# One projection stage by groups of 512 tokens, in place of two stages by tiles of 128

## The chip, the cores and the metric

The kernel runs on one core of a Trainium2 chip. The metric is the device time of one execution in microseconds (us). Engines are named as in the profile: PE is the matrix engine, PEld its weight loads, DVE the vector engine, ACT the scalar engine, POOL the general one, SP the queue that issues most transfers.

## What is computed

One layer of a decoder trunk: 2048 tokens of width 1024, token mixing, cross-attention to 256 memory tokens, a mixture of 32 experts, a final norm. All is float32. The change touches the projection ahead of the token mixing and the first of the two mixings:

```python
h = rmsnorm(x, norm_mix)              # (2048, 1024)
z = h @ w_in                          # (1024, 5 * 512): u, v_a, q, k, v
y_a = gelu(u) * (tril(w_s) @ rmsnorm(gelu(v_a), v_gain) + b_s)   # within chunks of 128 tokens, 4 groups of 128 channels
y_b = stick_breaking_attention(q, k, v)                          # 8 heads of 64, causal
x = x + concat(rmsnorm(y_a, out_norm_a), rmsnorm(y_b, out_norm_b)) @ w_out
```

## The kernel before

Every float32 product is made of three fp32r matmuls (`split_product`, L56 to L60): both operands are split into a high part (rounded to fp32r, by ACT) and a low part (the rest, by DVE), and high x high, high x low and low x high are added up in PSUM. A product of 128 tokens by 512 columns over the depth of 1024 is 8 x 3 = 24 matmuls of 128x512.

The work around the change stands in stages, each a block of its own with its own semaphores and an all-engine barrier behind it (`Scope.close`):

- `project_qkv` (L74 on) runs over 16 tiles of 128 tokens: load x, square (ACT), root (POOL), scale (DVE), 8 transposes of the normed tile (L286), split into `h_hi` and `h_lo`, then the products q, k and v with the tokens stationary and the weights moving. The result has tokens on the partitions, and the attention wants q and k with features there, so q and k are split, transposed head by head with both parts side by side (8 transposes at L315, 8 at L323), copied by ACT and DVE together and stored to DRAM by runs of 128 tokens. All 6 MB of the q, k and v weights are held, split, in SBUF.
- `mix_chunks` (L335 on) runs over the 16 tiles again: it loads and norms x, transposes (L598) and splits it a second time, makes the products u and v_a (the weights' 4 MB are loaded and cut at its start), gelu (ACT), the group norm (DVE, POOL), the spatial mix (4 matmuls at L614), gate, norm and store. The first loads of the attention (`StickLoads.load_first`) are issued near its end.
- `attend_stick` follows and loads q, k and v from DRAM by chunks of 512 tokens, with one transfer for each head of a pair.

Within a stage each engine has its order written out by hand, and waits on counting semaphores.

Of the kernel before, what the change touches and what calls it, by code (L numbers as in the profile page):

```python
# [6 lines left out]
ACT = mybir.ActivationFunctionType  # L7
# [13 lines left out]
class Scope:  # L21
# [15 lines left out]
    def two_views(self, name, shape):  # L37

        at = -(-self.nc.sbuf_base // 32) * 32
        cut = self.sbuf(name, shape, F32R)  # L40
        return cut, self.nc.alloc_sbuf_tensor_at(f"{self.stage}_{name}_raw", shape, F32, offset=at)
# [27 lines left out]
def project_qkv(nc, x, gain, w_in, ident, half, ident_bf, above, qt, kt, v):  # L69


    tokens, width = x.shape
    tiles, rows = tokens // P, width // P
    first_col = w_in.shape[1] - 3 * BANK  # L74
    heads, head_dim = qt.shape[0], qt.shape[1] // 2
    cols = w_in.shape[1] - first_col
    with ExitStack() as stack:
        s = Scope(nc, stack, "qkv")
        w_hi = s.sbuf("w_hi", [P, rows, cols], F32R)
        w_lo, w_raw = s.two_views("w_lo", [P, rows, cols])  # L80
        gains = s.sbuf("gains", [P, width])
        xs = s.sbuf("xs", [P, 2, width])
        hs = s.sbuf("hs", [P, 2, width])
        junk = s.sbuf("junk", [P, width], BF16)
        stat = s.sbuf("stat", [P, 2, 4])
        h_hi = s.sbuf("h_hi", [P, 2, rows, P], F32R)
        h_lo = s.sbuf("h_lo", [P, 2, rows, P], F32R)
        q_parts = s.sbuf("q_parts", [P, heads, 2, head_dim], F32R)
        k_parts = s.sbuf("k_parts", [P, heads, 2, head_dim], F32R)
        q_t = s.sbuf("q_t", [P, 2, heads, P], F32R)  # L90
        k_t = s.sbuf("k_t", [P, 2, heads, P], F32R)
        v_out = s.sbuf("v_out", [P, 2, BANK])
        ht_ps = s.psum("ht_ps", [P, rows, P])
        z_ps = s.psum("z_ps", [P, 3, BANK])
        t_ps = s.psum("t_ps", [P, heads, P])

        w_loaded = [[s.sem(f"w_loaded{c}_{r}") for r in range(rows)] for c in range(3)]
        filled, masked = s.sem("filled"), s.sem("masked")
        gains_loaded = s.sem("gains_loaded")
        w_hi_done, w_lo_done = s.sem("w_hi_done"), s.sem("w_lo_done")  # L100
        x_loaded = [s.sem(f"x_loaded{i}") for i in range(2)]
        squared, meaned, rooted, h_done = s.sem("squared"), s.sem("meaned"), s.sem("rooted"), s.sem("h_done")
        ht_done, hh_done, hl_done = s.sem("ht_done"), s.sem("hh_done"), s.sem("hl_done")
        zq_done, zk_done, zv_done = s.sem("zq_done"), s.sem("zk_done"), s.sem("zv_done")
        q_hi, q_lo, k_hi, k_lo = s.sem("q_hi"), s.sem("q_lo"), s.sem("k_hi"), s.sem("k_lo")
        qt_done, kt_done = s.sem("qt_done"), s.sem("kt_done")
        qt_act, qt_dve, kt_act, kt_dve = s.sem("qt_act"), s.sem("qt_dve"), s.sem("kt_act"), s.sem("kt_dve")
        v_done = s.sem("v_done")
        stored = [s.sem(f"stored{i}") for i in range(2)]
        half_heads = heads // 2  # L110

        with nc.Block() as block:
            @block.sync
            def _(sp):
                def load_x(t, slot):
                    sp.dma_start(xs[:, slot], x[bass.ds(t * P, P), :]).then_inc(x_loaded[slot], 16)

                def load_w(c):
                    for r in range(rows):
                        sp.dma_start(w_raw[:, r, c * BANK:(c + 1) * BANK],  # L120
                                     w_in[r * P:(r + 1) * P, first_col + c * BANK:first_col + (c + 1) * BANK]).then_inc(w_loaded[c][r], 16)

                load_x(0, 0)
                load_w(0)
                load_x(1, 1)
                load_w(1)
                load_w(2)

                def store(t, slot):
                    sp.wait_ge(qt_act, t + 1)  # L130
                    sp.wait_ge(qt_dve, t + 1)
                    sp.dma_start(qt[:, :, bass.ds(t * P, P)].rearrange("h p t -> p h t"), as_f32(q_t[:, slot])).then_inc(stored[slot], 16)
                    sp.wait_ge(v_done, t + 1)
                    sp.dma_start(v[bass.ds(t * P, P), :], v_out[:, slot]).then_inc(stored[slot], 16)
                    sp.wait_ge(kt_act, t + 1)
                    sp.wait_ge(kt_dve, t + 1)
                    sp.dma_start(kt[:, :, bass.ds(t * P, P)].rearrange("h p t -> p h t"), as_f32(k_t[:, slot])).then_inc(stored[slot], 16)

                with sp.Fori(0, tiles // 2 - 1) as j:
                    for slot in range(2):  # L140
                        sp.wait_ge(h_done, 2 * j + slot + 1)
                        load_x(2 * j + slot + 2, slot)
                        store(2 * j + slot, slot)
                for slot in range(2):
                    store(tiles - 2 + slot, slot)
                for slot in range(2):
                    sp.wait_ge(stored[slot], 16 * 3 * tiles // 2)

            @block.gpsimd
            def _(pool):  # L150
                def root(t, slot):
                    pool.wait_ge(meaned, t + 1)
                    nc.gpsimd.tensor_tensor(stat[:, slot, 2:3], stat[:, slot, 1:2], half[:, 0:1], ALU.pow).then_inc(rooted, 1)

                nc.gpsimd.memset(ident[:], 0.0).then_inc(filled, 1)
                nc.gpsimd.memset(half[:], -0.5).then_inc(filled, 1)
                nc.gpsimd.memset(ident_bf[:], 0.0).then_inc(filled, 1)
                nc.gpsimd.memset(above[:], 0.0).then_inc(filled, 1)
                pool.wait_ge(filled, 4)
                for tile, compare, fill in ((ident, ALU.not_equal, 1.0), (ident_bf, ALU.not_equal, 1.0), (above, ALU.is_gt, -1e30)):  # L160
                    nc.gpsimd.affine_select(out=tile[:], in_=tile[:], compare_op=compare, fill=fill, base=0,
                                            pattern=[[-1, P]], channel_multiplier=1).then_inc(masked, 1)
                root(0, 0)
                with pool.Fori(0, tiles // 2 - 1) as j:
                    root(2 * j + 1, 1)
                    root(2 * j + 2, 0)
                root(tiles - 1, 1)

            @block.scalar
            def _(act):  # L170
                def square(j, slot):

                    act.wait_ge(x_loaded[slot], 16 * (j + 1))
                    nc.scalar.activation(junk[:], xs[:, slot], ACT.Square, accum_out=stat[:, slot, 0:1]).then_inc(squared, 1)

                def high_h(t, slot):
                    act.wait_ge(ht_done, t + 1)
                    for part in range(2):
                        last = nc.scalar.copy(h_hi[:, slot, 4 * part:4 * part + 4], ht_ps[:, 4 * part:4 * part + 4])
                    last.then_inc(hh_done, 1)  # L180

                def cut_w(c):
                    for r in range(rows):
                        act.wait_ge(w_loaded[c][r], 16)
                        nc.scalar.copy(w_hi[:, r, c * BANK:(c + 1) * BANK], w_raw[:, r, c * BANK:(c + 1) * BANK]).then_inc(w_hi_done, 1)

                act.dma_start(gains[:], gain.partition_broadcast(P)).then_inc(gains_loaded, 16)
                square(0, 0)
                cut_w(0)
                high_h(0, 0)  # L190
                cut_w(1)
                cut_w(2)

                def tile(j, slot, last_tile=False):
                    t = 2 * j + slot
                    if not last_tile:
                        square(j + slot, 1 - slot)
                    act.wait_ge(zq_done, t + 1)
                    wait_past(act, qt_done, t)
                    nc.scalar.activation(q_parts[:, :, 0, :], z_ps[:, 0].rearrange("p (h d) -> p h d", h=heads),  # L200
                                         ACT.Copy, scale=head_dim ** -0.5).then_inc(q_hi, 1)
                    if not last_tile:
                        high_h(t + 1, 1 - slot)
                    act.wait_ge(zk_done, t + 1)
# [2052 lines left out]
```

## Time and profile before

| | us |
|---|---|
| median of 3 runs | 2894.77 (2889.86 to 2895.51) |
| profiled execution | 2895.18 |
| its span, first to last instruction | 2893.4 |
| `project_qkv`, first to last matmul or transpose | 9.6 to 334.3 |
| `mix_chunks`, first to last matmul | 351.1 to 585.0 |
| first matmul of the attention | 592.2 |

Over the span PE is busy for 91%, PEld 72%, DVE 52%, ACT 46% and POOL 22%, and PE's granted clock is 0.953 of full speed. Starts in the rows are counted from the first instruction. The end of a matmul in a row is modelled, so that neighbours overlap: what one costs is read from start to start.

### The profile page before, as it was taken

What the parts mean: (1) busy time and instruction counts of PE and PEld (TensorE: products, weight loads), DVE (VectorE), ACT (ScalarE), POOL (GpSimd) and SP (SyncE); (2) the same over time, 40 slices, a digit from 0 to 9 for tenths busy, and PEclk for the clock granted to TensorE, in tenths of its full rate; (3) what the DMA queues carried; (4) which work ended last, traced back from release to release, by engine and by line L of the source; (5) the groups of instructions that cost most, each with busy time, mean ns of one, the idle gap of its engine ahead of it and who ended that gap; (6) DMA issues with size and microseconds to landing.
All of it is one profiled execution on the core that took longest, in us unless ns stands there. A gap on an engine that the chain in (4) does not pass through costs nothing. (4 is left out here: it accounts for less than half of the span.)

```text
span 2893.4 us, 46489 instructions
## 1 busy us (share of the span) xinstructions
PE 2622.1 (91%) x14633; PEld 2095.4 (72%) x14635; DVE 1493.9 (52%) x1975; ACT 1316.4 (45%) x2332; POOL 629.1 (22%) x697
## 2 busy tenths in 40 slices
PE   7999689979999979978999999949999999999991
PEld 6888578856667657757678888737777788888880
DVE  4222245578888862220433333265788855555643
ACT  4222233278989961100322222124777755555642
POOL 0000011157777730000000000031222211112223
PEclk9999899989999989989999999959999999999995
DMA  4333411242021022232312221143999966666856
GB/s 167 94 91 94 135 61 59 62 89 67 16 67 49 2 88 98 101 141 104 114 53 78 87 80 59 66 170 118 372 372 367 355 217 210 208 213 219 282 152 249
DMA packets 203097, 406.93 MB, mean 141 GB/s; under 512 B 26096, under 2 KB 67568, under 8 KB 202992
## 3 DMA queue, kind: packets, MB, share of 16 engines
q1 hardware_dynamic: 186576, 363.04, 36.1%
q0 software_dynamic: 13968, 33.59, 5.0%
q10 hardware_dynamic: 2448, 8.91, 0.8%
q8 instruction: 64, 1.05, 0.2%
q14 instruction: 41, 0.34, 0.0%
HBM read 339.39 MB, written 83.36 MB: 146 GB/s over the span
## 5 line engine op out<-in xcount | busy, mean ns | idle before, releaser
L746 POOL TENSOR_TENSOR stick_weight<-stick_weight,stick_left 128x512 f32<-128x512 f32 (+3 forms) x320 | 327.9, 1038 | 127.0 <-DVE stick_left L874 122.6
L1625 DVE TENSOR_TENSOR moe_w_lo<-moe_w_lo_raw,moe_w_hi (+1 forms) x256 | 297.7, 1220 | 57.6 <-ACT moe_w_hi L1621 51.8
L1621 ACT CAST moe_w_hi<-moe_w_lo_raw (+1 forms) x256 | 255.2, 1054 | 39.3 <-DMA moe_w_lo_raw<-in_w 29.3
L874 DVE TENSOR_TENSOR_SCAN stick_left<-stick_z_ps,stick_left,stick_any_row 128x512 f32<-128x512 f32 x192 | 240.3, 1276 | 35.4 <-ACT stick_z_ps L837 35.1
L835 ACT ACTIVATE stick_weight<-stick_z_ps 128x512 f32<-128x512 f32 (+3 forms) x320 | 173.6, 542 | 32.7 <-PE stick_z_ps L784 21.1
L797 PE MATMUL stick_t_ps<-all_ident,stick_weight 128*128 128x128 f32 x1088 | 165.2, 281 | 18.8 <-ACT stick_weight_t L844 9.2
L58 PE MATMUL exp_g_ps<-moe_w_hi,exp_x_hi 128*128 x376 | 154.7, 411 | 22.0 <-DVE moe_w_lo L1625 11.1
L837 ACT ACTIVATE stick_z_ps<-stick_z_ps 128x512 f32<-128x512 f32 (+3 forms) x320 | 165.7, 518 | 10.4
L797 PEld LDWEIGHTS stick_t_ps<-all_ident,stick_weight 128*128 128x128 f32 x1088 | 116.1, 141 | 69.7 <-issue 45.6
L58 PE MATMUL qkv_z_ps<-qkv_w_hi,qkv_h_hi 128*128 128x512 f32 x384 | 157.5, 410 | 4.0 <-DVE qkv_h_lo L238 4.0
L58 PE MATMUL exp_y_ps<-moe_w_hi,exp_h_hi 128*128 128x512 f32 x376 | 153.5, 408 | 2.3 <-DVE exp_h_lo L2054 2.3
L2058 DVE TENSOR_TENSOR moe_w_lo<-moe_w_lo_raw,moe_w_hi 128x1024 f32 (+1 forms) x128 | 148.3, 1219 | 12.9 <-ACT moe_w_hi L2020 10.0
L59 PE MATMUL qkv_z_ps<-qkv_w_lo,qkv_h_hi 128*128 128x512 f32 x384 | 152.9, 398 | 0.0
L1636 POOL DMA_INDIRECT moe_xg<-hm_scratch,moe_now x50 | 60.6, 1212 | 423.1 <-PE exp_x_ps L2069 420.2
L60 PE MATMUL qkv_z_ps<-qkv_w_hi,qkv_h_lo 128*128 128x512 f32 x384 | 152.5, 397 | 0.0
L59 PE MATMUL exp_g_ps<-moe_w_lo,exp_x_hi 128*128 x376 | 150.1, 399 | 0.0
L60 PE MATMUL exp_g_ps<-moe_w_hi,exp_x_lo 128*128 x376 | 150.0, 399 | 0.0
L59 PE MATMUL exp_y_ps<-moe_w_lo,exp_h_hi 128*128 x376 | 149.4, 397 | 0.0
L60 PE MATMUL exp_y_ps<-moe_w_hi,exp_h_lo 128*128 128x512 f32 x376 | 149.3, 397 | 0.0
L58 PE MATMUL exp_u_ps<-moe_w_hi,exp_x_hi 128*128 x376 | 148.7, 395 | 0.0
L59 PE MATMUL exp_u_ps<-moe_w_lo,exp_x_hi 128*128 x376 | 148.7, 395 | 0.0
L60 PE MATMUL exp_u_ps<-moe_w_hi,exp_x_lo 128*128 x376 | 148.5, 395 | 0.0
(287 smaller groups left out, 5934.9 us busy)
## 6 DMA issues: line engine op xcount, KB each, us to landing
moe_w_lo_raw<-in_w SPq DMA_DIRECT2D x512, 256.0 KB
moe_w_lo_raw<-in_w SPq DMA_DIRECT2D x128, 512.0 KB
qkv_xs<-in_x SPq DMA_DIRECT2D x16, 512.0 KB, 4.7
qt_scratch<-qkv_q_t SPq DMA_DIRECT2D x16, 512.0 KB, 3.2
kt_scratch<-qkv_k_t SPq DMA_DIRECT2D x16, 512.0 KB, 3.5
gmlp_xs<-in_x SPq DMA_DIRECT2D x16, 512.0 KB, 3.7
mix_q<-qt_scratch SPq DMA_DIRECT2D x32, 256.0 KB
out_xs<-in_x SPq DMA_DIRECT2D x16, 512.0 KB, 3.4
```

Of the source, the lines that this page charges most:

```text
L58: pe.matmul(out, left_hi, right_hi, start=first, stop=False)
L59: pe.matmul(out, left_hi, right_lo, start=False, stop=False)
L60: return pe.matmul(out, left_lo, right_hi, start=False, stop=last)
L746: nc.gpsimd.tensor_tensor(taken, taken, after, ALU.mult).then_inc(weight_done, 1)
L797: last = nc.tensor.transpose(t_ps[:, n % 2, b], weight[:, n % W_SLOTS, b * P:(b + 1) * P], ident)
L835: nc.scalar.activation(weight[:, n % W_SLOTS, 0:keys], z, ACT.Sigmoid).then_inc(take_done, 1)
L837: nc.scalar.activation(z, z, ACT.Sigmoid, scale=-1.0).then_inc(leave_done, 1)
L874: nc.vector.tensor_tensor_scan(row[:, c * BANK:c * BANK + keys][:, ::-1], back, any_row[:, 0:keys], start, ALU.mult, ALU.bypass).then_inc( ...
L1621: nc.scalar.copy(self.w13_hi[:, self.w13_at(e, i)], self.w13_raw[:, self.w13_at(e, i)]).then_inc(self.w13_cut, 1)
L1625: ops.tensor_tensor(self.w13_lo[:, self.w13_at(e, i)], self.w13_raw[:, self.w13_at(e, i)], as_f32(self.w13_hi[:, self.w13_at(e, i)]), ALU. ...
L1636: nc.gpsimd.indirect_dma_start(out=self.xg[:], out_offset=None, in_=self.hm, in_offset=bass.IndirectOffsetOnAxis(ap=self.now[:].bitcast(U3 ...
L2058: nc.vector.tensor_tensor(w2_lo[:, w2_at(e, i)], w2_raw[:, w2_at(e, i)], as_f32(w2_hi[:, i]), ALU.subtract).then_inc(w2_ready, 1)
```

## The change

The two stages become one, `project`, without a loop: the order is a list of steps that every engine walks through.

- The steps are ("turn", t), the transposes and the split of tile t, and units, one product of 24 matmuls each. Tokens are taken by groups of 512 ("quads", 4 of them). `h_hi` and `h_lo` hold two quads.
- v is made by tokens as before. q and k are made by features: 128 columns of the weights are stationary and the 512 tokens move, so the result has features on the partitions, ACT and DVE split it straight into `qk_out`, and no transposes of q and k are left. Their scratch tensors are laid out by pairs of heads, and a store has runs of 512 tokens.
- A first pass makes q, k and v for all quads (48 units). The split tokens of quads 0 and 1 are written to DRAM on the way (`park`, 2 transfers of 2 MB for each quad); those of quads 2 and 3 stay.
- A gate pass makes u and v_a by tiles of 128 tokens (32 units) and the mixing, from quad 3 down to quad 0. It fetches the parked tokens again. x is loaded, normed and transposed once.
- The u and v_a weights are loaded over those of q and k during the first pass; those of v lie where the attention's first chunks come later (`room`). Products go round 4 PSUM banks.
- `StickLoads` loads both heads of a pair with one transfer over 128 partitions.

```diff
+    order = [("turn", 0), ("turn", 1)]
+    for a in range(per):
+        order.append((V, 0, a))
+        if a + 2 < per:
+            order.append(("turn", a + 2))
+    for quad in range(quads):
+        products = [(c, quad, f) for c in ((Q, K, V) if quad == quads - 1 else (Q, K) if quad == 0 else (V, Q, K)) for f in range(per)]
+        turns = [("turn", per * (quad + 1) + a) for a in range(per)] if quad < quads - 1 else []
+        for n, product in enumerate(products):
+            order.append(product)
+            if turns and n % (len(products) // per) == 0:
+                order.append(turns.pop(0))
+    gate_tiles = [per * quad + a for quad in range(quads - 1, -1, -1) for a in range(per)]
+    Z_SLOTS, X_SLOTS, OUT_SLOTS = 4, 3, 3
...
 SP, in the walk through the order
+                    if step == (K, quads - 1, 0):
+                        sp.wait_ge(z_done, number[(Q, quads - 1, per - 1)] + 1)
+                        load_w(U)
+                    if step == (V, quads - 1, 0):
+                        sp.wait_ge(z_done, number[(K, quads - 1, per - 1)] + 1)
+                        load_w(G)
...
+                    if n:
+                        store(n - 1)
+                    if step in ((Q, 0, 2), (Q, 1, 2)):
+                        park(step[1])
...
+                for m in range(tiles):
+                    if m == per:
+                        sp.wait_ge(z_done, n_units + 2 * per)
+                        sp.wait_ge(parked_out[1], 32)
+                        fetch(1)
...
 ACT
+                    if quad >= 2 and t % per == 0:
+                        act.wait_ge(z_done, 3 * per * (quad - 1))
+                        act.wait_ge(parked_out[quad % 2], 32)
...
+                square(0)
+                cut_w(V, range(rows // 2))
+                for step in order:
+                    if step[0] == "turn":
+                        t = step[1]
+                        high_h(t)
+                        if t == 0:
+                            cut_w(V, range(rows // 2, rows))
+                            square(1)
+                        if t + 2 < tiles:
+                            square(t + 2)
+                        if t == 2:
+                            cut_w(Q, range(rows))
+                        if t == 3:
+                            cut_w(K, range(rows))
+                        continue
+                    take(number[step])
+                    if step == (K, quads - 1, per - 1):
+                        cut_w(U, range(rows))
+                    if step == (V, quads - 1, 1):
+                        cut_w(G, range(rows))
...
 PE
-                    for h in range(heads):
-                        last = nc.tensor.transpose(t_ps[:, h], as_f32(q_parts[:, h].rearrange("p a d -> p (a d)")), ident)
-                    last.then_inc(qt_done, 1)
...
+                        last = split_product(nc.tensor, z_ps[:, n % Z_SLOTS], w_hi[i][:, r, cols], w_lo[i][:, r, cols],
+                                             h_hi[:, quad % 2, r], h_lo[:, quad % 2, r], r == 0, r == rows - 1)
...
+                for m, t in enumerate(gate_tiles):
+                    n, quad = n_units + 2 * m, t // per
+                    if quad < 2 and t % per == 0:
+                        pe.wait_ge(parked_in[quad % 2], 32)
+                    by_tokens(n, t, U, m == 0)
...
+                    by_tokens(n + 1, t, G, m == 0)
...
+                    if m:
+                        mix(m - 1)
```

ACT at the start, before. `xs` is the tile of x, `w_hi` the high part of the weights, `h_hi` that of the transposed tile:

```order
L174 ACTIVATE qkv_junk,qkv_stat<-qkv_xs 128x1024
L185 CAST qkv_w_hi<-qkv_w_lo_raw 128x512 x8
L179 CAST qkv_h_hi<-qkv_ht_ps 128x512 x2
L185 CAST qkv_w_hi<-qkv_w_lo_raw 128x512 x16
L174 ACTIVATE qkv_junk,qkv_stat<-qkv_xs 128x1024
L200 ACTIVATE qkv_q_parts<-qkv_z_ps 128x8x64
```

ACT at the start, in the change:

```order
L301 ACTIVATE proj_junk,proj_stat<-proj_xs 128x1024
L318 CAST proj_w_hi_54<-proj_w_lo_raw 128x512 x4
L311 CAST proj_h_hi<-proj_ht_ps 128x4x128 x2
L318 CAST proj_w_hi_54<-proj_w_lo_raw 128x512 x4
L301 ACTIVATE proj_junk,proj_stat<-proj_xs 128x1024 x2
L311 CAST proj_h_hi<-proj_ht_ps 128x4x128 x2
L301 ACTIVATE proj_junk,proj_stat<-proj_xs 128x1024
L326 COPY proj_v_out<-proj_z_ps 128x512
```

The first weights are cut in two halves around the first tile, and the tiles 1 and 2 are squared ahead of the other weights, which come between the first products.

PE at the seam between the two stages before: the last transposes of k, the transposes of the spatial weights, those of the first tile, and the first product of u.

```order
L60 MATMUL qkv_z_ps<-qkv_w_hi,qkv_h_lo 128x512
L323 MATMUL qkv_t_ps<-all_ident,qkv_k_parts 128x128 x8
...
L619 MATMUL gmlp_mix_ps<-all_ident,gmlp_ws_raw 128x128 x4
L598 MATMUL gmlp_ht_ps<-all_ident,gmlp_hs 128x128 x8
L58 MATMUL gmlp_z_ps<-gmlp_w_hi,gmlp_h_hi 128x512
```

PE at the seam between the two passes in the change, behind the first product of u:

```order
L67 MATMUL proj_z_ps<-proj_w_hi,proj_h_lo 128x512
L541 MATMUL proj_mix_ps<-all_ident,proj_ws_raw 128x128 x4
L65 MATMUL proj_z_ps<-proj_w_hi,proj_h_hi 128x512
L66 MATMUL proj_z_ps<-proj_w_lo,proj_h_hi 128x512
...
L519 MATMUL proj_mix_ps<-proj_v_norm,proj_ws_t 128x128 x4
```

Products stand right behind products here; only the 4 transposes of the spatial weights lie between.

SP's queue in the loop over the tiles, before:

```order
L116 DMA qkv_xs<-in_x 128x1024
L132 ISA
L132 DMA qt_scratch<-qkv_q_t 128x8x128
L134 ISA
L134 DMA v_scratch<-qkv_v_out 128x512
L137 DMA kt_scratch<-qkv_k_t 128x8x128
```

SP's queue around the first parking, in the change:

```order
L178 DMA proj_xs<-in_x 128x1024
L194 DMA qt_scratch<-proj_qk_out 128x2x512 x2
L200 DMA parked_scratch<-proj_h_hi 128x4096
L200 DMA parked_scratch<-proj_h_lo 128x4096
L178 DMA proj_xs<-in_x 128x1024
L194 DMA qt_scratch<-proj_qk_out 128x2x512 x2
```

The two large stores stand between the store of one q unit and the next load of x.

## Rows read from the trace of the kernel before

**Rows 1.** By stretch: length, busy us of PE, PEld, DVE, ACT, POOL; clock, DMA, GB/s

```profile
15.50:333.50 318.00, 313.19 (x1523) 257.80 (x1523) 92.66 (x139) 86.03 (x153) 8.21 (x15) 0.99 0.32 96
333.50:369.30 35.80, 3.93 (x21) 2.92 (x19) 14.72 (x16) 15.13 (x19) 1.72 (x3) 0.54 0.69 235
369.30:576.50 207.20, 207.20 (x1000) 170.82 (x1001) 106.91 (x217) 58.34 (x115) 30.55 (x43) 0.99 0.17 55
576.50:592.20 15.70, 3.15 (x17) 2.66 (x16) 6.81 (x17) 2.21 (x6) 2.29 (x5) 0.68 0.09 34
```

**Rows 2.** Waits of PE until 592 us: total, times, longest

```profile
PE gmlp_mix_ps L619 <- POOL gmlp_ws_raw L450: 16.8, 1, 16.8
...
PE gmlp_z_ps L58 <- DVE gmlp_h_lo L536: 14.4, 1, 14.4
```

**Rows 3.** Timeline of the start: start, length, engine, line [idle before, releaser]

```profile
7.15 5.25 ACT L185 CAST qkv_w_hi<-qkv_w_lo_raw 128x512 fp32r<-128x512 f32 x8
...
9.61 1.94 PE L286 MATMUL qkv_ht_ps<-all_ident,qkv_hs 128*128 128x128 f32 x8 [9.61 <-DVE qkv_hs L231]
12.31 1.07 ACT L179 CAST qkv_h_hi<-qkv_ht_ps 128x512 fp32r<-128x512 f32 x2
...
15.54 0.80 PE L58 MATMUL qkv_z_ps<-qkv_w_hi,qkv_h_hi 128*128 128x512 f32 x1 [3.98 <-DVE qkv_h_lo L238]
...
24.44 1.05 ACT L174 ACTIVATE qkv_junk<-qkv_xs 128x1024 bf16<-128x1024 f32 x1
...
27.78 1.97 PE L286 MATMUL qkv_ht_ps<-all_ident,qkv_hs 128*128 128x128 f32 x8 [4.78 <-DVE qkv_hs L231]
29.40 0.78 PE L58 MATMUL qkv_z_ps<-qkv_w_hi,qkv_h_hi 128*128 128x512 f32 x1
```

**Rows 4.** Timeline of PE in `project_qkv`: one product and the transposes behind it

```profile
153.82 0.48 PE L58 MATMUL qkv_z_ps<-qkv_w_hi,qkv_h_hi 128*128 128x512 f32 x1
154.14 0.39 PE L59 MATMUL qkv_z_ps<-qkv_w_lo,qkv_h_hi 128*128 128x512 f32 x1
154.37 0.39 PE L60 MATMUL qkv_z_ps<-qkv_w_hi,qkv_h_lo 128*128 128x512 f32 x1
...
159.50 1.03 PE L323 MATMUL qkv_t_ps<-all_ident,qkv_k_parts 128*128 128x128 f32 x8
```

**Rows 5.** Timeline of PE at the seam of the two stages

```profile
333.28 1.03 PE L323 MATMUL qkv_t_ps<-all_ident,qkv_k_parts 128*128 128x128 f32 x8
...
369.27 0.76 PE L58 MATMUL gmlp_z_ps<-gmlp_w_hi,gmlp_h_hi 128*128 128x512 f32 x1 [14.36 <-DVE gmlp_h_lo L536]
...
377.13 1.04 PE L598 MATMUL gmlp_ht_ps<-all_ident,gmlp_hs 128*128 128x128 f32 x8
```

**Rows 6.** Timeline of PE in `mix_chunks`: from one spatial mix to the next

```profile
434.62 1.05 PE L614 MATMUL gmlp_mix_ps<-gmlp_v_norm,gmlp_ws_t 128*128 128x128 f32 x8
...
441.13 1.03 PE L598 MATMUL gmlp_ht_ps<-all_ident,gmlp_hs 128*128 128x128 f32 x8
441.92 0.48 PE L58 MATMUL gmlp_z_ps<-gmlp_w_hi,gmlp_h_hi 128*128 128x512 f32 x1
...
447.60 1.05 PE L614 MATMUL gmlp_mix_ps<-gmlp_v_norm,gmlp_ws_t 128*128 128x128 f32 x8
```

**Rows 7.** Timeline of PE from the last product to the attention

```profile
576.52 1.05 PE L614 MATMUL gmlp_mix_ps<-gmlp_v_norm,gmlp_ws_t 128*128 128x128 f32 x8
...
592.21 0.90 PE L784 MATMUL stick_z_ps<-mix_k_first,mix_q 64*128 64x128 f32 x6 [7.27 <-PEq L32]
```

**Rows 8.** Transfers: all loads of x until 60 us; stores of q (KB, us to landing)

```profile
DMA to landing us min/median/max: 4.7/6.4/9.8
...
qt_scratch<-qkv_q_t SPq DMA_DIRECT2D x16, 512.0 KB, 3.2
```

**Rows 9.** By stretch, as rows 1: two stretches with the DMA engines full

```profile
0.00:20.00 20.00, 6.41 (x20) 5.14 (x22) 12.00 (x21) 13.98 (x24) 2.04 (x12) 1.00 0.92 335
...
600.00:620.00 20.00, 17.39 (x172) 12.23 (x172) 16.28 (x21) 17.89 (x44) 13.38 (x15) 1.00 0.97 196
```

More of the change, by code:

```diff
@@ new lines, in project @@
+    quads = tiles // per
+    pairs, head_dim = qt.shape[0], qt.shape[2] // 2
+    U, G, Q, K, V = range(5)
+    slot_of = {V: 2, Q: 0, K: 1, U: 0, G: 1}
+    cut_order = [V, Q, K, U, G]
+    order = [("turn", 0), ("turn", 1)]
[10 more added lines that the diff above has]
+                order.append(turns.pop(0))
@@ L380, in mix_chunks @@
[L380 to L384 removed]
+        w_loaded = [[s.sem(f"w_loaded{i}_{r}") for r in range(rows)] for i in range(3)]
@@ new lines, in _ @@
+                for tile, compare, fill in ((ident, ALU.not_equal, 1.0), (ident_bf, ALU.not_equal, 1.0), (above, ALU.is_gt, -1e30)):
+                    nc.gpsimd.affine_select(out=tile, in_=tile, compare_op=compare, fill=fill, base=0,
+                                            pattern=[[-1, P]], channel_multiplier=1).then_inc(masked, 1)
+                for t in range(tiles):
+                    pool.wait_ge(meaned, t + 1)
+                    nc.gpsimd.tensor_tensor(stat[:, t, 2:3], stat[:, t, 1:2], half[:, 0:1], ALU.pow).then_inc(rooted, 1)
@@ new lines, in _ @@
+                dve.wait_ge(gains_loaded, 16)
+                norm(0)
+                cut_w(V, range(rows // 2))
+                for step in order:
+                    if step[0] == "turn":
+                        t = step[1]
+                        low_h(t)
+                        if t == 0:
+                            cut_w(V, range(rows // 2, rows))
+                            norm(1)
+                        if t + 2 < tiles:
+                            norm(t + 2)
+                        if t == 2:
+                            cut_w(Q, range(rows))
+                        if t == 3:
+                            cut_w(K, range(rows))
+                        continue
+                    take(number[step])
+                    if step == (K, quads - 1, per - 1):
+                        cut_w(U, range(rows))
+                    if step == (V, quads - 1, 1):
+                        cut_w(G, range(rows))
@@ new lines, in by_tokens @@
+                def by_tokens(n, t, c, first):
+                    i, quad = slot_of[c], t // per
+                    bank_free(n)
+                    for r in range(rows):
+                        if first:
+                            pe.wait_ge(w_lo_done, cut_order.index(c) * rows + r + 1)
+                        last = split_product(nc.tensor, z_ps[:, n % Z_SLOTS], h_hi[:, quad % 2, r, in_quad(t)], h_lo[:, quad % 2, r, in_quad(t)],
+                                             w_hi[i][:, r], w_lo[i][:, r], r == 0, r == rows - 1)
+                    last.then_inc(z_done, 1)
```

737 lines of the change are left out of this document (285 added, 452 removed).

## Prediction

> **What bounds the kernel now.** I read first the busy time by stretch [rows 1], to see where PE is idle between the first instruction and the attention's first matmul at 592.2 us. In the first stage it is busy for 313 of 318 us and in the second for 207.2 of 207.2: both are bound by PE, with DVE at 29% and 52% and ACT at 27% and 28%. Between them lie 35.8 us with 3.9 us of PE, and behind them 15.7 us with 3.2 us. Then the waits of PE [rows 2]: two of them make up nearly all of the seam, 16.8 us until the spatial weights are masked and 14.4 us until the first tile is split, which stands behind the cutting of the new weights on DVE. So three things are worth something here: matmuls that go, the seam, and the start. Work taken from ACT, DVE or the DMA queues inside the stages is worth nothing.
>
> Then the price of PE's pieces, from start to start. A matmul of 128x512 takes 0.23 us (154.14 to 154.37). A product of 24 of them behind a group of small matmuls takes 159.50 - 153.82 = 5.68 us, of which 0.09 is its first step (0.32 in place of 0.23): 5.59 us where it stands behind another product [rows 4]. Eight transposes take 441.92 - 441.13 = 0.79 us, with the slow first step behind them 0.88. The spatial mix (4 matmuls of two rows each) costs 0.81 + 0.09 = 0.90. A tile of the second stage repeats after 447.60 - 434.62 = 12.98 us = 2 x 5.59 + 0.88 + 0.90 [rows 6]. The pieces add up.
>
> **The change, part by part.** I lay out PE's new order in time with these prices and compare the start of the second to last mix, 576.52 us [rows 7].
>
> *Number of matmuls.* q and k by features: 4 groups of features x 4 quads x 24 = 384 each; by tokens it was 16 x 24 = 384. Nothing changes there, nor in v, u and v_a: 80 products in all. Each matmul has its own weight load before and after, and both orders change the stationary operand two times in three. I take 5.59 us for both kinds.
>
> *q and k transposes go.* 32 groups x 0.88 = 28.2 us, all on the path. The copies behind them (ACT, DVE) go too, at no gain. The last of these groups borders on the seam and is counted there.
>
> *The second norm and transposes go.* 16 groups of 8: 15 on the path x 0.88 = 13.2 us, one in the seam.
>
> *The seam goes.* From the last k transposes to the first product of u it is 369.27 - 333.28 = 36.0 us, and that product takes 377.13 - 369.27 = 7.86 us in place of 5.68, since the granted clock has fallen meanwhile (0.54 in this stretch) [rows 1, 5]. In the change the products of u follow those of v. What covers the weights: u's are cut behind (K, 3, 3), with all of v of quad 3 (22.4 us) still to be done, against 5.25 us of cutting for 8 pieces on ACT [rows 3]. The load of the v_a weights starts at the end of (K, 3, 3) too; 2 MB took about 9.8 us at the start at worst [rows 8]; ACT comes to them behind (V, 3, 1), 11.2 us on, and is done by about 17.5, DVE by 18.6; they are wanted after 22.4 + 5.6 = 28 us. The margin is 9 us. If that cover fails, the stall is what exceeds it. The transposes of the spatial weights cost 0.5 us. Seam: 36.0 + 2.2 - 0.5 = 37.7 us.
>
> *The start.* Before, the first product starts at 15.54 us. Now PE's order has turn 1 ahead of it. ACT: half of the cuts until 7.15 + 2.6 = 9.8 us; the first transposes end at 11.55; high part 1.07 us, to 12.7; the other half, to 15.3; the square of tile 1. From a square's start to its transposes it took 27.78 - 24.44 = 3.34 us, and from those to the product 29.40 - 27.78 = 1.62 [rows 3]. So turn 1 starts at 18.7 and the first product at 20.3, 4.8 us later than before. x of tile 1 is issued at about 5.6 us and lands at 15.4 by the slowest row [rows 8], just in time. At the slow clock the first product takes up to 7.86 us (the row of the seam): end at 28.2. In return the second product waits no more: before, PE was idle for 4.78 us and transposed slowly at 27.78 [rows 3]. Then V 0, turn 2, V 1, turn 3, V 2, V 3: the cuts for q (ACT from about 31 to 37 us) are wanted at 47, those of k at 69. x of tile 3 is queued behind 6 MB of weights, lands at about 15.6 + 9.8 = 25.4 us and is wanted at 34.
>
> *Sum.* End of the first product 28.2; 79 more x 5.59 = 441.6; 14 turns x 0.88 = 12.3; spatial transposes 0.5; 14 mixes x 0.90 = 12.6: the second to last mix starts at 495.2 us against 576.5. The gain is 81.3 us. The tail of 15.7 us is the same chain (group norm, mix, gate, norm, store, barrier) and stays [rows 7].
>
> *What is queued where.* Evictions: a q or k unit costs ACT 0.6 and DVE 0.7 us of 5.6, and 4 banks give PE three more units. SP: the load of x for tile t + 3 stands behind a store that waits for the unit before. A load took 4.7 to 9.8 us [rows 8], and the tile is wanted two turns later, at least 11 us.
>
> *Parking.* This is the part without a row. 4.2 MB are written for quad 0, and again for quad 1, then read twice. Nearest rows: all engines full at 335 GB/s and at 196 GB/s [rows 9]; a store of 512 KB in 3.2 us with its latency, 164 GB/s [rows 8]. That is 12.5, 21 or 25.6 us. On the way out the cover is the queue behind it: the store of (Q, 0, 2) lands late, its slot of `qk_out` is wanted by (K, 0, 1) on ACT, and PE can still go on to (V, 1, 0), 7 units and 3 turns = 41.7 us after (Q, 0, 1), less 1.4 of eviction and 3.2 for the store itself: 37 us. On the way in it is 4 tiles of the gate pass, 4 x 12.1 = 48 us. So it costs nothing at either end. I take the middle, 21 us, since stores are no faster than loads in any row.
>
> The Trainium skill speaks against it, in "DMA: Bandwidth & Descriptors", section "Latency and other measured facts": copies of 16 KiB per partition ran at 207 GB/s and fell to 103 GB/s at large row pitches that are powers of two; it advises contiguous tiles. Here a row of a parked tensor is 16 KiB and the next follows at once. By the bad figure 4.2 MB would be an estimated 41 us. No run here shows such a transfer yet.
>
> *Attention's loads.* One transfer over 128 partitions in place of two over 64. In the stretch where they keep the DMA engines full PE is busy for 17.39 of 20 us, and they move 196 GB/s against 335 at the start [rows 9]. A gain of up to 2.6 us (what PE is idle there), or nothing. I take nothing and keep 2.6 for the range; a loss has no reason, for the bytes and the runs of 2 KB are the same.
>
> **The rivals.**
> - *Parking at half rate.* At half of 196 GB/s a quad takes 43 us; the outward cover of 37 us fails by 6 us, twice: 12 us, so 2826 us. For it: the store of (Q, 0, 2) and the next x stand behind it in one queue. Against it: no stretch with full DMA is under 196 GB/s [rows 9]. The rule of the Trainium skill above comes out at nearly this case: by its 41 us it would be 4 us twice, 2822 us.
> - *Stalls from the in-order queues.* ACT and DVE walk through one list: where ACT waits for an x that is queued behind 6 MB, `take` and the next split wait too. If tile 3 lands 15 us later than I say, turn 2's split is late by as much and PE stops once, for up to 10 us; if the v_a cuts are late, as much again. For it: before, the second tile's chain cost 4.8 us at this place. Against it: margins of 9 us in each. Price 8 to 20 us, so 2822 to 2834.
> - *Slower than before.* One mechanism: the parked transfers are slow enough. The stall is 2 x (T - 37) + 2 x (T - 48) for T us each; it eats the 81.3 us from T = 63 us on, under 67 GB/s. At 50 GB/s (T = 84) it is 166 us: 2980. For it: no row has a transfer of this shape. Against it: 67 GB/s is a third of the slowest full stretch [rows 9].
> - *More than forecast.* The attention's start gains 2.6 us and the first product is less cold: 2809 to 2811.
>
> **How the numbers follow.** The profiled execution took 2895.2 us; less 81.3 it is 2813.9. It lies 0.4 us over the median of the runs shown, so the median falls to about 2813.5; I say 2814. Chances: forecast, with 2809 to 2819 for the small terms, 0.75; stalls in queues 0.13; half rate 0.05; more than forecast 0.05; slower 0.02. The range takes in the half rate, most of the stalls and the gain at the attention, and 3 us on either side for the spread of the runs (2889.9 to 2895.5): 2806 to 2830. A measurement of this kernel can tell about 0.2%, 6 us: faster 0.97, same 0.01, slower 0.02.
>
> **What would show it.** In the profile after: one stretch from about 20 to 495 us in which PE has no wait over 1 us and a clock of 1.00; first product at 20 us; the first pass ends near 303 us and a gate tile repeats after 2 x 5.59 + 0.90 = 12.1 us; the spacing of products by features is 0.23 us; the attention's first matmul at about 511 us. Wrong if PE waits for `h_lo` or a bank behind (Q, 0, 2) (parking), if it waits at the 8th gate tile (fetch), if there is a gap at the seam (cuts), or if matmuls with the weights stationary are spaced wider: 0.01 us more on 768 of them is 7.7 us.

## The result, and the profile after

| | before | after |
|---|---|---|
| median of 4 runs, us | 2893.73 (2889.86 to 2895.51) | 2801.11 (2800.46 to 2801.26) |
| ratio, 95% interval | | 0.9681 (0.9664 to 0.9698) |
| span of the profiled execution | 2893.4 | 2799.3 |
| first product | 15.54 | 20.04 |
| second to last spatial mix | 576.52 | 482.81 |
| first matmul of the attention | 592.21 | 498.43 |
| from there to the end | 2301.2 | 2300.9 |

The change gains 92.6 us where 81.3 were forecast, and 2801 lies below the range that was given. All of it is gained ahead of the attention: 93.8 us there, 0.3 behind it. (Those two come from the profiled executions; the one of before lies 1.5 us over its median.) By stretch (columns as rows 1), with cuts at the first product, behind the first product of u, behind the last product and at the attention:

```profile
0.00:20.00 20.00, 3.52 (x16) 3.17 (x18) 9.89 (x17) 10.08 (x18) 3.16 (x14) 1.00 0.92 337
20.00:300.90 280.90, 280.90 (x1290) 233.64 (x1289) 79.05 (x121) 75.86 (x137) 7.79 (x14) 1.00 0.44 153
300.90:482.80 181.90, 181.90 (x862) 152.59 (x860) 70.67 (x160) 28.68 (x59) 23.00 (x29) 1.00 0.19 74
482.80:498.40 15.60, 3.14 (x17) 2.64 (x16) 6.81 (x17) 2.20 (x6) 2.29 (x5) 0.66 0.09 34
498.40:518.40 20.00, 18.06 (x144) 11.94 (x144) 13.86 (x20) 17.32 (x44) 11.43 (x17) 0.84 0.82 263
```

PE is busy for 280.90 of 280.90 us and for 181.90 of 181.90, and the row gives the full clock (only the first eight matmuls of the first product are slow, 0.43 us apart): the stretch of [rows 1] with 3.93 of 35.8 us is gone. The waits of PE until 520 us (total, times, longest) hold the start and the tail and nothing between:

```profile
PE proj_ht_ps L478 <- DVE proj_xs L379: 16.5, 2, 9.6
...
PE stick_z_ps L694 <- PEq L32: 7.2, 1, 7.2
...
PE proj_mix_ps L519 <- DVE proj_v_norm L466: 5.3, 1, 5.3
```

So no other wait went: the surprise must lie in busy time. The timeline of PE (start, length) at the start, at the seam and at the end, as rows 3, 5 and 7:

```profile
20.04 0.78 PE L65 MATMUL proj_z_ps<-proj_w_hi,proj_h_hi 128*128 128x512 f32 x1
...
27.27 1.04 PE L478 MATMUL proj_ht_ps<-all_ident,proj_xs 128*128 128x128 f32 x8
...
295.54 0.39 PE L65 MATMUL proj_z_ps<-proj_w_hi,proj_h_hi 128*128 128x512 f32 x1
...
300.99 0.60 PE L541 MATMUL proj_mix_ps<-all_ident,proj_ws_raw 128*128 128x128 f32 x4
301.34 0.48 PE L65 MATMUL proj_z_ps<-proj_w_hi,proj_h_hi 128*128 128x512 f32 x1
...
471.02 1.05 PE L519 MATMUL proj_mix_ps<-proj_v_norm,proj_ws_t 128*128 128x128 f32 x8
...
482.81 1.05 PE L519 MATMUL proj_mix_ps<-proj_v_norm,proj_ws_t 128*128 128x128 f32 x8
```

The first product of u starts at 295.54 us, where the first pass was forecast to end near 303, and a gate tile repeats after 482.81 - 471.02 = 11.79 us, where 12.1 was forecast. Both say that a product costs less than was taken. The reason is in the spacing of the big matmuls within one product:

```profile
100.19 0.39 PE L65 MATMUL proj_z_ps<-proj_w_hi,proj_h_hi 128*128 128x512 f32 x1
100.42 0.39 PE L66 MATMUL proj_z_ps<-proj_w_lo,proj_h_hi 128*128 128x512 f32 x1
100.65 0.39 PE L67 MATMUL proj_z_ps<-proj_w_hi,proj_h_lo 128*128 128x512 f32 x1
100.87 0.39 PE L65 MATMUL proj_z_ps<-proj_w_hi,proj_h_hi 128*128 128x512 f32 x1
```

Three of them take 100.87 - 100.19 = 0.68 us, 0.227 each. Averaged over the whole stage the spacing is 227 ns, by tokens and by features alike (226.7 to 227.0 for each line and operand); before, the average over both stages is 233 ns, which [rows 4] show rounded, as 0.23. The blocks below give 226.67 and 233.33 for the two; on 1920 matmuls the 6.6 ns between them are 12.7 us, as much as was missed (the second to last mix came 495.2 - 482.8 = 12.4 us early). But why does the same matmul cost less? The instruction is the same, the number of weight loads too. That is what most experiments are about.

### The profile page after: what moved, and what is told of

Its sections match the earlier page's. It is cut to its first block and busy times, and to the rows that moved or that the text cites. A ratio compares the mean times of both kernels' runs of the same rounds, so it can differ in the third digit from the quotient of the medians.

```text
span 2799.3 us, 44924 instructions
## 1 busy us (share of the span) xinstructions
PE 2560.8 (91%) x14249; PEld 2049.6 (73%) x14251; DVE 1432.3 (51%) x1887; ACT 1262.0 (45%) x2244; POOL 619.9 (22%) x681
## 5 line engine op out<-in xcount | busy, mean ns | idle before, releaser
L65 PE MATMUL proj_z_ps<-proj_w_hi,proj_h_hi 128*128 128x512 f32 x384 | 151.9, 396 | 0.0
L66 PE MATMUL proj_z_ps<-proj_w_lo,proj_h_hi 128*128 128x512 f32 x384 | 150.2, 391 | 0.0
L67 PE MATMUL proj_z_ps<-proj_w_hi,proj_h_lo 128*128 128x512 f32 x384 | 150.0, 391 | 0.0
```

The source lines that it names most:

```text
L65: pe.matmul(out, left_hi, right_hi, start=first, stop=False)
L66: pe.matmul(out, left_hi, right_lo, start=False, stop=False)
L67: return pe.matmul(out, left_lo, right_hi, start=False, stop=last)
```

## The experiments

Spacings are from start to start averaged over the steady part of a block, since a single row rounds them to 10 ns. The time of before was taken beside each batch: 2894.3, 2894.9 and 2894.0 us.

### probe_layout: is it the program, or where the operands lie?

Behind the end of the changed kernel, 12 blocks of 6 plain products each, with nothing beside them. They differ only in the addresses that the operands are read from, and one of them in the PSUM bank:

```diff
+    # name: moving hi, lo, elements from row to row; stationary hi, lo, elements from row to row; bank
+    configs = [("old", 22688, 71840, 1536, 143552, 151744, 128, 2),
+               ("new", 22688, 39072, 512, 120992, 153760, 512, 2),
+               ("new_hrow", 22688, 39072, 512, 120992, 153760, 128, 2),
...
+               ("new_hat", 22688, 39072, 512, 121024, 153792, 512, 2),
...
+                                pe.matmul(z_ps[:], wh, mh, start=r == 0, stop=False)
+                                pe.matmul(z_ps[:], wh, ml, start=False, stop=False)
+                                last = pe.matmul(z_ps[:], wl, mh, start=False, stop=r == rows - 1)
```

> The changed kernel, with a block of plain products behind its end: 12 settings, each 6 products of 24 fp32r matmuls of 128x512 with no waits between them, on constant data. The settings differ in where the operands lie in SBUF. The spacing of matmuls in the trace was 0.2335 us before (mean over the q, k, v products) and 0.2267 us in the changed kernel, for products by tokens and by features alike. Theory A, the place: the spacing goes by addresses or by the elements from one row of the depth to the next, of the moving or the stationary operand. Then the setting with the old places gives about 0.2335, the one with the new places 0.2267, and the settings that change one of the two at a time show which. Theory B, the program: the spacing goes by what stands around the matmuls (waits, loops, the order of the stationary parts). Then all settings give the same spacing, whichever it is. The time as a whole grows by about 12 x 42 us + 12 x 7 us of barriers + 60 us of filling, 650 us.

The time of 3246 us says nothing; the spacings do:

| block | what is taken from where | ns |
|---|---|---|
| old | all as in `project_qkv` of before | 233.33 |
| new | all as in the changed kernel, by tokens | 226.67 |
| feat | as in the changed kernel, by features | 226.67 |
| new_hrow, new_wrow | new, with one row step of old | 226.67 |
| old_wrow, old_hrow | old, with one row step of new | 233.33 |
| old_bank | old, another PSUM bank | 233.33 |
| new_hat | new, stationary operand 32 bytes on | 233.33 |
| old_hat | old, stationary operand 32 bytes on (64 out of line) | 233.33 |
| new_at0 | new, all four parts shifted by -32 bytes | 226.66 |
| old_at0 | old, the moving operand alone shifted by -32 bytes (64 out of line) | 233.33 |

Timeline of PE in block `new`, and in `new_hat`:

```profile
2869.89 0.39 PE L2157 MATMUL new_z_ps<-probe_room 128*128 128x512 f32 x1
2870.11 0.39 PE L2158 MATMUL new_z_ps<-probe_room 128*128 128x512 f32 x1
2870.34 0.39 PE L2156 MATMUL new_z_ps<-probe_room 128*128 128x512 f32 x1
2870.57 0.39 PE L2157 MATMUL new_z_ps<-probe_room 128*128 128x512 f32 x1
...
2970.68 0.40 PE L2157 MATMUL new_hat_z_ps<-probe_room 128*128 128x512 f32 x1
2970.91 0.40 PE L2158 MATMUL new_hat_z_ps<-probe_room 128*128 128x512 f32 x1
2971.15 0.40 PE L2156 MATMUL new_hat_z_ps<-probe_room 128*128 128x512 f32 x1
2971.38 0.40 PE L2157 MATMUL new_hat_z_ps<-probe_room 128*128 128x512 f32 x1
```

Three steps are 0.68 us in the first and 0.70 in the second. Both of the kernels' prices come back with no other work beside them, so neither DMA traffic nor the evictions make the difference. It isn't the row step and isn't the bank (another one was tried for the old places alone): it is the place of the stationary operand, and 32 bytes are enough.

### probe_shift: which places are good?

The same probe from the addresses of `new`, with the operands shifted one way or another.

> The changed kernel with plain products behind its end, 12 settings of 6 products as in the first probe. There the spacing was 0.2268 us where moving and stationary operands start at the same address modulo 512 bytes, and 0.2333 us where they differ by 32 or 64 bytes (both at a multiple of 64, or neither, made no difference). Now the stationary operands alone are moved by 0, 16, 32, 64, 96, 128, 256 and 480 bytes, then the high stationary part alone by 32, the low one alone, the low moving part alone, and all four together. Theory A, equal modulo 512: only 0 and all four together are at 0.2268. Theory B, equal modulo 128 or 256: those of 128 (and 256) are as well. Theory C, the start of a transfer of 64 bytes: 64, 128 and 256 as well; the first probe speaks against it. With one part alone out of line A expects values between, since one or two matmuls in three meet a distance.

| what is shifted | ns |
|---|---|
| both stationary parts, by 0 or 256 bytes | 226.67 |
| by 16, 32, 64 or 480 | 233.33 |
| by 96 | 234.32 |
| by 128 | 232.45 |
| only the high, only the low stationary part, by 32 | 231.9, 233.33 |
| only the low moving part, by 32 | 231.67 |
| all four, by 32 | 226.67 |

So it is not an alignment of its own: shifting all four together costs nothing. What counts in these blocks is that the moving and the stationary operand start at the same place modulo 256 bytes of a partition; what was expected beforehand was modulo 512, and the shift by 256 bytes, which costs nothing, speaks against it. In `project_qkv` of before the weights start at 22688 and 71840 bytes (160 modulo 256), the tokens at 143552 (192): 32 bytes out of line. In the changed kernel all of them leave 160. The diff says nothing of it; it follows from which buffers stand ahead of the tokens. Why the hardware does it, no run says.

### after_out_of_line and before_in_line: the same in the kernels

If this is the whole miss, 32 bytes of padding in the changed kernel must give it back, and padding in before must bring it there too.

```diff
+        s.sbuf("pad", [P, 8])
         h_hi = s.sbuf("h_hi", [P, 2, rows, BANK], F32R)
```

> The changed kernel with 32 bytes of padding ahead of the split tokens, so that they lie 32 bytes off the weights modulo 512 in all 80 products. Nothing else changes. If the place of the operands is the whole of what my forecast missed, the spacing goes from 0.2267 back to about 0.2333 us, 1920 x 0.0066 = 12.7 us are lost, and the time is 2801.1 + 12.7 = 2813.8, which is the forecast. Rival: the padding costs less than half of that (the reason is in the program, and the probe's plain products don't carry over): under 2807.

It took 2812.76 us (2810.74 to 2813.71; ratio 0.9718, 0.9704 to 0.9731): 11.7 us more for eight unused numbers per partition, and within 1.0 us of the forecast. Its timeline of PE:

```profile
101.05 0.40 PE L65 MATMUL proj_z_ps<-proj_w_hi,proj_h_hi 128*128 128x512 f32 x1
101.29 0.39 PE L66 MATMUL proj_z_ps<-proj_w_lo,proj_h_hi 128*128 128x512 f32 x1
101.52 0.39 PE L67 MATMUL proj_z_ps<-proj_w_hi,proj_h_lo 128*128 128x512 f32 x1
101.75 0.40 PE L65 MATMUL proj_z_ps<-proj_w_hi,proj_h_hi 128*128 128x512 f32 x1
```

Three steps are 0.70 us again, and the attention starts at 510.19 us, where the prediction had it (511).

```diff
         stat = s.sbuf("stat", [P, 2, 4])
+        s.line_up("line_up", weights_at)
         h_hi = s.sbuf("h_hi", [P, 2, rows, P], F32R)
```

`line_up` puts in as much padding as makes the next buffer start where the weights do, modulo 512 bytes; it stands in both stages of before.

> The kernel before, with 352 to 480 bytes of padding ahead of the split tokens in its two stages, so that they start at the same address modulo 512 as the weights. 1920 matmuls; if their spacing goes from 0.2333 to 0.2267 us it is 12.7 us faster, less what the short groups between the products take back (some 8 matmuls behind each are at 0.231 to 0.236): 9 to 12.7 us, 2881 to 2885. Rival: in this kernel with its short groups the spacing never settles; under 4 us.

It took 2882.84 us (2880.28 to 2883.3; ratio 0.9955, 0.9941 to 0.9969), 12.1 us less than before. The attention starts at 580.11 us instead of 592.21. With this the result splits in two: the change without the layout is worth 2882.8 - 2801.1 = 81.7 us in line, and 2894.93 - 2812.76 = 82.2 out of line, for 81.3 forecast; the layout is worth 12.

### turns_back: what the transposes of q and k cost

Eight transposes of the identity are put back behind each of the 32 products by features.

```diff
                         by_features(number[step])
+                        for g in range(2 * groups):
+                            nc.tensor.transpose(mix_ps[:, g % groups], ident, ident)
```

> The changed kernel with 8 transposes of the identity behind each of the 32 products by features, into a PSUM bank that is free then: what the transposes of q and k cost PE, without their copies. By the prediction 32 x 0.88 = 28.2 us more than the changed kernel, so 2829. Rival: the small group also makes the matmuls behind it slower (0.2335 in place of 0.2267 us over a whole product of 24), as the groups stood in every product of the kernel before and seldom stand in the new one: then 32 x 24 x 0.0068 = 5.2 us more on top, 2834.5.

2828.91 us (2827.4 to 2831.5; ratio 0.9774). The attention starts at 526.93 us, 28.5 later, for 32 x 0.88 = 28.2. The timeline shows one group of them with a turn and a product behind it:

```profile
64.12 1.03 PE L533 MATMUL proj_mix_ps<-all_ident 128*128 128x128 f32 x8
64.99 1.04 PE L478 MATMUL proj_ht_ps<-all_ident,proj_xs 128*128 128x128 f32 x8
65.78 0.48 PE L65 MATMUL proj_z_ps<-proj_h_hi,proj_w_hi 128*128 128x512 f32 x1
66.10 0.39 PE L66 MATMUL proj_z_ps<-proj_h_lo,proj_w_hi 128*128 128x512 f32 x1
```

From 64.12 to 64.99 it is 0.87 us; the turn behind it takes 0.79, and the first matmul of a product 0.32 in place of 0.23.

### no_park and park_out_x4: is the parking free?

In `no_park` nothing is parked or fetched: the gate pass of quads 0 and 1 reads the tokens of quads 2 and 3 again, so that what is computed from there on differs.

```diff
-                    if step in ((Q, 0, 2), (Q, 1, 2)):
-                        park(step[1])
...
-                        sp.wait_ge(parked_out[1], 32)
-                        fetch(1)
```

> The changed kernel without parking: quads 0 and 1 of split tokens are neither written out nor fetched, so the gate pass computes with the tokens of quads 2 and 3 in their place. Theory A (my step in the prediction): parking is hidden at both ends, its 4.2 MB took 13.6 us out and 12.7 us in against covers of 37 and 48 us; the time stays within 1 us of the changed kernel. Rival: part of the transfers' traffic slows PE or a load; then this kernel is 2 to 8 us faster than the changed one.

The run took 2832.17 us (ratio 0.9784), which is no answer to the question: other tokens are routed to other experts (each form of the experts' product matmuls runs 392 times in place of 376), and what follows the attention's first matmul takes 2334.3 us in place of 2300.9. The stage itself can be compared. The last matmul of its last product starts at 481.87 us, against 482.58, but the second product had already started at 27.34 us against 28.06. From there on both take the same, 454.53 and 454.52 us: the parking costs nothing.

`park_out_x4` writes each parked quad four times, to four places, and waits for all.

```diff
-                        sp.dma_start(parked[quad, part], as_f32(h[:, quad % 2].rearrange("p r t -> p (r t)"))).then_inc(parked_out[quad % 2], 16)
+                        for copy in range(4):
+                            sp.dma_start(parked[copy, quad, part], as_f32(h[:, quad % 2].rearrange("p r t -> p (r t)"))).then_inc(parked_out[quad % 2], 16)
```

> The changed kernel with each outward transfer of the parking done four times, to four places; fetched once. Out they take about 4 x 13 = 52 us. By the prediction's cover of 37 us (the slot of the output buffer that the third unit behind wants, and four PSUM banks) PE stops for about 15 us at each of two places: 30 us more than the changed kernel, so 2831. Rival, no cover model: stores and loads of x overtake in the 16 engines, PE does not stop: within 2 us of the changed kernel. Other rival: the cover is shorter, since the load of x for a turn stands behind the parking too and the turns come first: 50 us or more.

2830.12 us (2826.97 to 2830.5; ratio 0.9774), and the attention starts 28.6 us later. The waits of PE until 520 us show where:

```profile
PE proj_ht_ps L479 <- DVE proj_h_lo L387: 23.7, 2, 12.0
```

Twice 12 us, for `h_lo`: the wait that the prediction named for a parking that is too slow; the clock falls to 0.50 meanwhile, and the slow matmuls behind each wait (0.43 us apart) make up the rest of the 28.6. The way to it was the prediction's only once. Behind the second parking ACT stood for 30.7 us before the slot of `qk_out`, behind the first for 27.7 us before a tile of x whose load stood behind the stores. The transfers of the changed kernel (KB, us to landing), out and in:

```profile
parked_scratch<-proj_h_hi SPq DMA_DIRECT2D x2, 2048.0 KB, 8.3
parked_scratch<-proj_h_lo SPq DMA_DIRECT2D x2, 2048.0 KB, 13.1
...
proj_h_hi<-parked_scratch SPq DMA_DIRECT2D x2, 2048.0 KB, 7.8
proj_h_lo<-parked_scratch SPq DMA_DIRECT2D x2, 2048.0 KB, 12.7
```

Both parts of a quad are issued together, so 4.2 MB are through in 13.1 us: 320 GB/s, with covers of 37 and 48 us.

### weights_late: what the cover of the new weights is worth

The loads and the cuts of u's and v_a's weights wait for the end of the last product of v, as before the change.

```diff
-                    if step == (K, quads - 1, 0):
-                        sp.wait_ge(z_done, number[(Q, quads - 1, per - 1)] + 1)
-                        load_w(U)
...
+                sp.wait_ge(z_done, n_units)
+                load_w(U)
+                load_w(G)
...
-                    if step == (K, quads - 1, per - 1):
+                    if step == (V, quads - 1, per - 1):
                         cut_w(U, range(rows))
-                    if step == (V, quads - 1, 1):
                         cut_w(G, range(rows))
```

> The changed kernel with the loads of the u and v_a weights issued only behind the last product of the first pass, and cut there. Theory: the seam is hidden by the products of v of quad 3 and by nothing else. Then PE stops from the last product of v until the first piece is loaded (4.7 to 9.8 us by the loads in the traces) and cut (1.3 us), is paced by the cuts of 0.66 us a piece for the first product, and runs some 10 matmuls at the slow clock (2.2 us): 8 to 13 us more than the changed kernel, 2809 to 2814. Rival: the products of v hide little, since the v_a weights' cuts run beside the first product of u in any case: under 4 us.

2806.74 us (2805.17 to 2807.18; ratio 0.9698): 5.6 us more, less than the 8 to 13 of the theory and more than the rival's 4. Its timeline and its stretches (columns as rows 1):

```profile
294.60 0.39 PE L67 MATMUL proj_z_ps<-proj_w_hi,proj_h_lo 128*128 128x512 f32 x1
299.19 0.77 PE L65 MATMUL proj_z_ps<-proj_w_hi,proj_h_hi 128*128 128x512 f32 x1 [4.21 <-DVE proj_w_lo L390]
299.76 0.63 PE L66 MATMUL proj_z_ps<-proj_w_lo,proj_h_hi 128*128 128x512 f32 x1
300.18 0.63 PE L67 MATMUL proj_z_ps<-proj_w_hi,proj_h_lo 128*128 128x512 f32 x1
```

```profile
294.90:299.20 4.30, 0.09 (x2) 0.04 (x1) 0.71 (x2) 1.82 (x3) 0.00 (x0) 0.93 0.69 208
299.20:305.30 6.10, 6.10 (x14) 4.75 (x15) 5.00 (x8) 4.66 (x8) 0.00 (x0) 0.50 1.03 367
```

PE waits for 4.2 us, and behind that the granted clock is 0.50, the lower of the two levels, for 6.1 us. 14 matmuls are 0.43 apart there where 0.227 would do, some 2.8 us more. Together that is 7.0 us. The first product of u starts at 299.19 us in place of 295.54, and the product behind it is 307.99 - 301.34 = 6.65 late, in an execution whose second product had started 0.7 us earlier. The forecast took the wait too long: it had 4.7 to 9.8 us for the load of the first piece, and ACT began to cut it 297.71 - 295.01 = 2.7 us after the first load was issued.

### after_in_line_all and start_first: can more be had?

The output projection, the cross attention and the experts of both kernels have products of the same kind, spaced 233.1 to 233.3 ns in the changed kernel. `after_in_line_all` has `line_up` there too.

```diff
         stat = s.sbuf("stat", [P, 2, 4])
+        s.line_up("line_up", weights_at)
         y_hi = s.sbuf("y_hi", [P, 2, rows, P], F32R)
```

> The changed kernel, with padding in the output projection, the cross-attention and the expert stage too, so that all their split products have moving and stationary operands equal modulo 512. Their matmuls are spaced 0.2333 us on average now. Output projection 768 matmuls, 5.1 us; cross-attention 1536, 10.1 us; experts 3384, up to 22.3 us where PE sets the pace. If all are on the path it is 37.5 us faster, 2764; if the experts go by their weights' transfers (DMA 71% and PE 88% busy there) only the first two, 15 us: 2786. Rival: no gain outside the probed shapes, 2801.

2776.07 us (2774.04 to 2777.57; ratio 0.959, 0.9577 to 0.9604): 25.0 us less than the changed kernel, between the two forecasts. First to last product of a stage, from the traces: output projection 203.5 us for 208.7, cross attention 494.9 for 505.8, experts 861.9 for 873.4. The first two give about what their 768 and 1536 matmuls x 6.6 ns say (5.1 and 10.1 us), the experts half of 3384 x 6.6 = 22.3. It isn't that their operands stayed out of line: their spacing falls from 233.3 to 227.5 ns too, which is 17.4 us over the steps from one such matmul to the next. But PE then waits longer for the cutting of the next weights, in the changed kernel and here:

```profile
PE exp_g_ps L65 <- DVE moe_w_lo L1535: 11.4, 11, 1.1
...
PE exp_g_ps L71 <- DVE moe_w_lo L1546: 17.4, 12, 1.5
```

That takes 6.0 of the 17.4 us back, and leaves the 11.5 measured.

`start_first` adds another order of the first steps: the first product stands ahead of turn 1.

```diff
-    order = [("turn", 0), ("turn", 1)]
...
+    order = [("turn", 0), (V, 0, 0), ("turn", 1), ("turn", 2), (V, 0, 1), ("turn", 3), (V, 0, 2), (V, 0, 3)]
```

> The changed kernel with all operands in line, as after_in_line_all (2776.1), and the first product of v ahead of the turn of tile 1: turn 0, V 0, turn 1, turn 2, V 1 in place of turn 0, turn 1, V 0, turn 2, V 1. The first product then starts when tile 0 is split, at about 14.5 us in place of 20.0, ends at 22, and PE waits once for the split of tile 1 (turn 1 until 23, split until 25.5); V 1 starts at about 26.3 in place of 28.1: 1.8 us faster, 2774. Rival: two waits at a slow clock take the place of one, no gain or up to 3 us lost.

2773.28 us (2773.16 to 2775.22; ratio 0.9586, 0.9573 to 0.96), close to the 2774 that was expected and the lowest time of all, but its interval overlaps that of `after_in_line_all`: by the times the two can't be told apart. The last product starts 1.1 us earlier in the trace. Waits of PE until 482 us, here:

```profile
PE proj_ht_ps L480 <- DVE proj_xs L381: 9.6, 1, 9.6
PE proj_z_ps L71 <- DVE proj_h_lo L388: 3.9, 2, 2.5
PE proj_ht_ps L480 <- DVE proj_h_lo L388: 2.6, 1, 2.6
```

They add up to 16.1 us, where `after_in_line_all` has 16.4 in two waits, for the tiles 0 and 1. The product starts at 13.98 us, 6 earlier, and PE waits behind it instead.

## Why the prediction was right and wrong

- **Matmuls that go: right.** The 32 groups of q and k cost 28.5 us when they are put back, for 28.2. The 81.7 us between the kernels, both in line, leave no other error in the sum larger than the spread of the runs, unless two of them cancel.
- **The seam goes: right.** PE has no wait there. The first product of u starts at 295.5 us where the first pass was to end at 303, and the 47 cheaper products (47 x 0.15 = 7.1 us) and 0.9 at the first one account for that, to 0.3 us. That the early loads and cuts make it so is shown by `weights_late`, but only for a part: of the 37.7 us, 5.6 come back when loads and cuts alone are late. The rest is then the spatial weights' 16.8 us and the first tile's split [rows 2], both of which are no longer there to wait for. That is read from the rows and was not tried by itself.
- **The start: right.** 20.04 us for 20.3. The first product took 27.27 - 20.04 = 7.23 us, for up to 7.86; with the rounding of its start that is 0.9 of the miss.
- **The tail: right.** 498.43 - 482.81 = 15.6 us, for 15.7.
- **Parking: right, with the price too high.** 13.1 us to land, for 21 taken from bounds of 12.5 and 25.6. It was free: `no_park` runs the stage in the same time. The Trainium skill, in "DMA: Bandwidth & Descriptors", section "Latency and other measured facts", gives 103 GB/s for copies at row pitches of 4 and 8 MiB, and advises to lay tiles out contiguously. The 16 KiB rows here follow one another directly, so the 41 us that the prediction worked out from that figure took it beyond the case that it is stated for; the transfer ran at 320 GB/s.
- **Attention's loads: right to take nothing.** In its first 20 us the DMA engines moved 263 GB/s in place of 205, but PE was busy for 18.06 us of them in place of 18.20, and what follows took 2300.9 us for 2301.2. The transfers got faster, PE did not wait for them less.
- **Wrong: the term "79 more x 5.59".** The failed step is "I take 5.59 us for both kinds". That both kinds cost the same was right, that the price of before holds for after was not: a product costs 24 x 0.2267 = 5.44 us. 79 x 0.15 = 11.9 us, and 0.9 at the first product, are the 12.4 us by which the second to last mix came earlier (495.2 - 482.8), to 0.4. The prediction saw that this price is multiplied by 1920, but allowed it to move only upwards, and only for the 768 by features. On the lower side the range held 3 us for the spread of the runs and nothing for this price; what a different layout can do to it, some 12 us, was no term at all.

None of the four rivals came about. "More than forecast" had the right sign, but from the attention and the first product's clock, which gave 0.3 and 0.9 us.

## What to carry to other kernels

A price that is multiplied by thousands must be read to the nanosecond over hundreds of instructions, not from two rows rounded to 0.01 us, and a change that moves buffers may change it. Where PE sets the end with a run of matmuls like these, look at where the moving and the stationary operand start modulo 256 bytes; padding of under 512 bytes per partition gained 12 us in the two stages of before and 25 us in the later stages of the changed kernel. Where another engine works just ahead of PE, as at the experts' weights, part of such a gain turns into waiting. Where a run leaves out work that later steps depend on, compare the stage itself and not the time.

## What the runs showed of the hardware

- 128x512 matmuls in fp32r with a weight load each are spaced 226.67 ns when both operands start at the same place modulo 256 bytes of a partition, 231.7 to 234.3 ns in all other cases tried (shifts of 16, 32, 64, 96, 128 and 480 bytes, of both or of one part). At the full clock of 2.4 GHz that is 544 cycles and, for most, 560. The row steps tried (128 and 512 elements stationary, 512 and 1536 moving) and another PSUM bank made no difference. Other shapes and types, and the attention, were not tried.
- A wait of 4.2 us behind a long busy stretch was followed by 6.1 us at half the clock (0.50), with PE busy all the time.
- Two stores of 2 MB with contiguous 16 KiB rows landed after 8.3 and 13.1 us, the fetches after 7.8 and 12.7: loads and stores of this form run alike.
